# First stage of a hybrid decoder step: x in four column quarters, two weight groups in turn

## The reference

```python
def trunk_layer(x, lw, mlstm_fn, conv_fn):
    xn = rmsnorm(x, g_mix)
    z = xn @ w_in + b_in
    zq, zk, zv, zi, zf, zo, zu, zc, zb, zga, zgb = jnp.split(z, _split_points(), axis=-1)
    ...
    h, m_state = mlstm_fn(q, k, v, ig, lf)
    h_a = jax.nn.sigmoid(zo) * h
    conv_out, conv_state = conv_fn(zc * zu, w_conv)
    y_b = zb * conv_out
    merged = jax.nn.sigmoid(zga) * (h_a @ p_a) + jax.nn.sigmoid(zgb) * (y_b @ p_b)
    x = x + merged @ w_o
    u = jax.nn.relu(rmsnorm(x, g_ffn) @ w_up)
    x = x + (u * u) @ w_down
```

## Time and profile before

| | |
|---|---|
| Median of 3 runs | 1912.51 us (1912.1 to 1912.95) |
| Profiled execution, span | 1911.0 us |
| PE busy | 1889.9 us (99%) |
| PEld busy | 1855.8 us (97%) |
| DVE busy | 941.6 us (49%) |
| ACT busy | 689.5 us (36%) |
| Share of PE in the chain that ended last | 98% |
| PE busy in the first 20 us / the second 20 us | 9.12 us / 19.79 us |

### The profile page before, as it was taken

The page is one execution under the profiler, slowest core; times in us unless marked ns, Lnnn a source line. Parts: engine busy times, 40 slices in busy tenths (PEclk is TensorE's granted clock), DMA queues, the critical chain, the costliest instruction groups (busy, mean ns, idle before and its releaser), DMA issues.

```text
span 1911.0 us, 33610 instructions
## 1 busy us (share of the span) xinstructions
PE 1889.9 (99%) x12647; PEld 1855.8 (97%) x12647; DVE 941.6 (49%) x1045; ACT 689.5 (36%) x825; POOL 34.5 (2%) x67
## 2 busy tenths in 40 slices
PE   7999999999999999999999999999999999999998
PEld 7999898989899999999999999999999999999997
DVE  6565545454454444445555544455444544455544
ACT  5344343434343333333443333333333333333331
POOL 1001000010100000000000000000000000000000
PEclk9999999999999999999999999999999999999998
DMA  7446564756465545544454444444444444444442
GB/s 208 144 127 190 132 213 133 220 119 216 138 177 146 151 143 155 152 148 148 143 172 156 140 159 145 151 150 141 160 145 151 150 147 154 143 154 151 145 155 78
DMA packets 294469, 293.86 MB, mean 154 GB/s; under 512 B 12506, under 2 KB 292314, under 8 KB 294300
## 3 DMA queue, kind: packets, MB, share of 16 engines
q1 hardware_dynamic: 283464, 282.67, 48.8%
q10 hardware_dynamic: 10692, 9.51, 1.6%
q0 software_dynamic: 272, 1.12, 0.1%
HBM read 281.10 MB, written 12.17 MB: 153 GB/s over the span
## 4 chain that ended last, share of the span: by engine, by line
PE 98%; DVE 1%; DMA 0%; issue 0%; ACT 0%; SPq 0%; DVEq 0%; ACTq 0%
PE ps L1250 97%; DVE y_out L1243 0%; PE ps L1350 0%; DMA x_tok<-in_x_sample_dram 0%; PE ps L1270 0%; DVE x_low L840 0%; DVE x_T L843 0%; PE ps L1507 0%; DVE w_low L823 0%; ACT x_high L561 0%; PE ps L1451 0%; DVE sq_acc L1216 0%; DVE x_T L1212 0%; ACT tmp L790 0%; DVEq L110 0%
## 5 line engine op out<-in xcount | busy, mean ns | idle before, releaser
L823 DVE TENSOR_TENSOR w_low<-raw,w_high 128x1024 fp32r<-128x1024 f32 x512 | 621.7, 1226 | 609.0 <-ACT w_high L543 605.1
L543 ACT ACTIVATE w_high<-raw 128x1024 fp32r<-128x1024 f32 x512 | 534.9, 1055 | 712.5 <-PE ps L1250 709.1
L1250 PE MATMUL ps<-x_high,w_high 128*128 128x320 f32 (+2 forms) x2432 | 755.5, 311 | 1.3 <-PE ps L1250 1.1
L1250 PE MATMUL ps<-x_low,w_high 128*128 128x320 f32 (+2 forms) x2432 | 755.8, 311 | 0.0
L1250 PE MATMUL ps<-x_high,w_low 128*128 128x320 f32 (+2 forms) x2432 | 753.2, 310 | 0.0
L1250 PEld LDWEIGHTS ps<-x_high,w_high 128*128 128x128 f32 x2432 | 457.5, 188 | 7.2 <-issue 4.6
L1250 PEld LDWEIGHTS ps<-x_high,w_low 128*128 128x128 f32 x2432 | 458.6, 189 | 0.0
L1250 PEld LDWEIGHTS ps<-x_low,w_high 128*128 128x128 f32 x2432 | 457.3, 188 | 0.1
L1250 PE MATMUL ps<-u_high,w_high 128*128 128x320 f32 x1024 | 316.5, 309 | 0.0
L1250 PE MATMUL ps<-u_low,w_high 128*128 128x320 f32 x1024 | 316.4, 309 | 0.0
L1250 PE MATMUL ps<-u_high,w_low 128*128 128x320 f32 x1024 | 316.4, 309 | 0.0
(11 more groups left out here) (250 smaller groups left out, 1160.2 us busy)
## 6 DMA issues: line engine op xcount, KB each, us to landing
raw<-in_w_in_dram SPq DMA_DIRECT2D x176, 512.0 KB, 3.8
raw<-in_w_up_dram SPq DMA_DIRECT2D x128, 512.0 KB, 3.9
raw<-in_w_down_dram SPq DMA_DIRECT2D x128, 512.0 KB, 3.4
raw<-in_w_o_dram SPq DMA_DIRECT2D x32, 512.0 KB, 3.5
C_state<-in_state_mlstm_C_dram SPq DMA_DIRECT2D x16, 512.0 KB, 6.5
raw<-in_state_mlstm_C_dram SPq DMA_DIRECT2D x16, 512.0 KB, 4.1
out_dram<-C_state ACTq DMA_DIRECT2D x8, 1024.0 KB, 6.8
raw<-in_p_a_dram SPq DMA_DIRECT2D x16, 512.0 KB, 4.3
```

Source lines behind the costliest of these rows:

```text
L543: a.activation(wh[:, s % RING], raw[:, s % RING], ACT.Copy).then_inc(high_done, 1)
L823: v.tensor_tensor(wl[:, s % RING], raw[:, s % RING], wh[:, s % RING].bitcast(F32), ALU.subtract).then_inc(low_done, 1)
L1250: return pe.matmul(out, lhsT, rhs, start=start, stop=stop)
```

## The change

- SP loads x in four column quarters (672 KB each, five DMAs). Order: quarter 0, weights of units 0 and 1, quarter 1, units 2 and 3, quarters 2 and 3, units 4 and 5, the small rows, units 6 and 7. 
- The first convolution's units alternate: units 0 and 1 are row part 0 of zu and of zc, units 2 and 3 row part 1, and so on. Both accumulators are filled at the same time. XBANKS moves to the banks 4 to 7, the transposed vectors to ACC[0].
- PE: transposes of quarter 0, unit 0, transposes of quarter 1, units 1 and 2, quarter 2, units 3 and 4, quarter 3, units 5 and 6, columns, scales, unit 7.
- ACT: x_high of a quarter, splits and sums of squares in the written order below; its first instruction is x_high, no longer a sum.
- DVE: x_low of a quarter, then a split, then the plain copies x_T of that quarter.
- The four gate loads are issued by POOL instead of SP.

The diff, cut to its core:

```diff
@@ -230,7 +230,10 @@
         ACC = [ps[:, 0:2, :], ps[:, 2:4, :], ps[:, 6:8, :]]
         M = [ps[:, 4 + n, :] for n in range(4)]
         HEAD_ACC = [0, 1, 0, 1, 2]
-        XBANKS = [ACC[1], ACC[2]]
+        XBANKS = [ps[:, 4:6, :], ps[:, 6:8, :]]
+        XQ = 4
+        XB = KB // XQ
+        assert XQ == NU and XB == UK
 
         YPARTS = [(0, 0), (0, 1), (0, 2), (1, 0), (1, 1), (0, 3), (1, 2), (1, 3), (2, 0), (2, 1), (2, 2), (2, 3)]
         YBANK = [5, 6, 7, 0, 1, 2, 3]
...
@@ -361,10 +364,10 @@
 
         @block.sync
         def _(sp):
-            def tokens(half):
-
-                c = slice(D // 2 * half, D // 2 * half + D // 2)
-                in0, in1, in2 = s_xtok[3 * half:3 * half + 3]
+            def tokens(quarter):
+
+                c = slice(D // XQ * quarter, D // XQ * (quarter + 1))
+                in0, in1, in2 = s_xtok[3 * quarter:3 * quarter + 3]
                 sp.dma_start(xtok[0:NMETA, 0, c], meta[:, c]).then_inc(in0, 16)
                 sp.dma_start(xtok[NMETA:P, 0, c], x_prompt[0, 0:P - NMETA, c]).then_inc(in0, 16)
                 sp.dma_start(xtok[:, 1, c], x_prompt[0, P - NMETA:2 * P - NMETA, c]).then_inc(in1, 16)
...
@@ -391,15 +396,15 @@
                 sp.dma_start(crows[:], state_conv[0].rearrange("b r c -> (b r) c")).then_inc(s_brows, 16)
                 sp.dma_start(nrows[:], state_n[0].rearrange("b h d -> (b h) d")).then_inc(s_brows, 16)
 
-            def gates():
-                sp.dma_start(gw[:], w_in[0, :, CG:CG + 32].rearrange("(k p) n -> p k n", p=P)).then_inc(s_gw, 16)
-                with nc.allow_non_contiguous_dma(reason="40 numbers"):
-                    sp.dma_start(bi[:], b_in[0, CG:CG + H].rearrange("(h o) -> h o", o=1)).then_inc(s_small, 16)
-                    sp.dma_start(bf[:], b_in[0, CG + H:CO].rearrange("(h o) -> h o", o=1)).then_inc(s_small, 16)
-                    sp.dma_start(m0[:], state_m[0].rearrange("b h -> h b")).then_inc(s_small, 16)
-
             tokens(0)
-            convolution(0, {1: lambda: tokens(1), 3: small, 4: gates})
+            first_convolution(range(0, 2))
+            tokens(1)
+            first_convolution(range(2, 4))
+            tokens(2)
+            tokens(3)
+            first_convolution(range(4, 6))
+            small()
+            first_convolution(range(6, UCV))
             with sp.Fori(1, H) as i:
                 convolution(i)
             with sp.Fori(0, H) as h:
...
@@ -499,6 +511,7 @@
                 pool.wait_ge(s_pick, n + 2)
                 g.affine_select(out=pick[:], in_=pick[:], compare_op=ALU.not_equal, fill=1.0, base=-32 * n,
                                 pattern=[[-1, H]], channel_multiplier=1).then_inc(s_pick, 1)
+            gates()
             pool.wait_ge(s_row, 9)
             with nc.allow_non_contiguous_dma(reason="36 stabilisers"):
                 pool.dma_start(m_prompt.rearrange("l b h -> h (l b)"), mrw[:, TP - 1:TP]).then_inc(s_mout, 16)
@@ -545,26 +558,19 @@
             def sum_squares(half, n):
 
                 nt, done = (P, P, NMETA + TS)[n], 3 * half + n
-                act.wait_ge(s_xtok[done], 16 if n == 1 else 32)
+                for quarter in range(XQ // 2 * half, XQ // 2 * (half + 1)):
+                    act.wait_ge(s_xtok[3 * quarter + n], 16 if n == 1 else 32)
                 if done > 0:
                     act.wait_ge(s_sq, done)
                 a.activation(squares[0:nt, 0:D // 2], xtok[0:nt, n, D // 2 * half:D // 2 * half + D // 2], ACT.Square,
                              accum_out=spart[0:nt, half, n:n + 1]).then_inc(s_sq, 1)
 
-            act.wait_ge(s_set, 1)
-            for n in range(2):
-                sum_squares(0, n)
-
-            act.wait_ge(s_col, 1)
-            for k in range(KB):
-                act.wait_ge(s_xtr, k // 2 + 1)
-                a.activation(xh[:, k, :], XBANKS[k // 2 % 2][:, k % 2, 0:T], ACT.Copy,
-                             scale=vecT[:, VG + k:VG + k + 1]).then_inc(s_xh, 1)
-                if k % 4 == 3 and k // 4 < LEAD:
-                    split(0, k // 4)
-                    if k < 4:
-                        sum_squares(0, 2)
-                    sum_squares(1, k // 4)
+            def x_high(quarter):
+
+                for k in range(XB * quarter, XB * (quarter + 1)):
+                    act.wait_ge(s_xtr, k // 2 + 1)
+                    a.activation(xh[:, k, :], XBANKS[k // 2 % 2][:, k % 2, 0:T], ACT.Copy,
+                                 scale=vecT[:, VG + k:VG + k + 1]).then_inc(s_xh, 1)
 
             def root():
                 act.wait_ge(s_ms, 2)
...
@@ -611,7 +623,32 @@
                              ACT.Exp).then_inc(s_rowa, 1)
                 a.activation(wkr[:], wkr[:], ACT.Exp).then_inc(s_rowa, 1)
 
-            convolution(0, {1: root, 2: gate_weights, 3: lambda: act.wait_ge(s_col, 2)})
+            act.wait_ge(s_col, 1)
+            x_high(0)
+            split(0, 0)
+            split(0, 1)
+            x_high(1)
+            split(0, 2)
+            act.wait_ge(s_set, 1)
+            for n in range(3):
+                sum_squares(0, n)
+            split(0, 3)
+            x_high(2)
+            split(0, 4)
+            x_high(3)
+            split(0, 5)
+            for n in range(3):
+                sum_squares(1, n)
+            split(0, 6)
+            gate_weights()
+            split(0, 7)
+            root()
+            split(0, 8)
+            split(0, 9)
+            act.wait_ge(s_col, 2)
+            bias_u(0)
+            split(0, 10)
+            bias_c(0)
             with act.Fori(1, H - 1) as i:
                 convolution(i)
             convolution(H - 1, {1: log1p_exp, 4: row_exps})
...
@@ -835,14 +872,17 @@
                 dve.wait_ge(seen, n + 4)
 
 
-            for k in range(KB):
-                dve.wait_ge(s_xh, k + 1)
-                v.scalar_tensor_tensor(xl[:, k, :], XBANKS[k // 2 % 2][:, k % 2, 0:T], vecT[:, VG + k:VG + k + 1],
-                                       xh[:, k, :].bitcast(F32), ALU.mult, ALU.subtract).then_inc(s_xl, 1)
-                if k % 2 == 1:
-                    v.tensor_copy(xT[:, k - 1:k + 1, T0:T], XBANKS[k // 2 % 2][:, :, T0:T]).then_inc(s_xT, 1)
-                if k % 4 == 3 and k // 4 < LEAD:
-                    split(0, k // 4)
+            def x_low(quarter):
+
+                for k in range(XB * quarter, XB * (quarter + 1)):
+                    dve.wait_ge(s_xh, k + 1)
+                    v.scalar_tensor_tensor(xl[:, k, :], XBANKS[k // 2 % 2][:, k % 2, 0:T], vecT[:, VG + k:VG + k + 1],
+                                           xh[:, k, :].bitcast(F32), ALU.mult, ALU.subtract).then_inc(s_xl, 1)
+
+            def x_plain(quarter):
+
+                for k in range(XB * quarter, XB * (quarter + 1), 2):
+                    v.tensor_copy(xT[:, k:k + 2, T0:T], XBANKS[k // 2 % 2][:, :, T0:T]).then_inc(s_xT, 1)
 
             def columns():
                 dve.wait_ge(s_colT, 2)
@@ -884,14 +924,14 @@
             scale_z = rbc[:, TZ0:T].unsqueeze(1).to_broadcast([P, GB, TZ])
             scale_o = rbc[:, T0:T].unsqueeze(1).to_broadcast([P, GB, TO])
 
-            def convolution(i, extra=()):
-                for p in range(UCV):
+            def convolution(i, extra=(), begin=0, ends=(3, 7)):
+                for p in range(begin, UCV):
                     split(UCV * i, p + LEAD)
                     if p in extra:
                         extra[p]()
-                    if p in (3, 7):
-                        g = p // 4
-                        dve.wait_ge(unit_used, RING + UCV * i + 4 * g + 4)
+                    if p in ends:
+                        g = ends.index(p)
+                        dve.wait_ge(unit_used, RING + UCV * i + p + 1)
                         if g == 0:
                             dve.wait_ge(s_z, 1 + i)
                             dve.wait_ge(s_cv, 1 + 12 * i)
@@ -980,7 +1020,14 @@
                 row(v.tensor_copy(decr[:], rows[:, RWI:RWI + TS].rearrange("p (b t) -> p b t", t=DS)
                                   [:, :, DS - 1]))
 
-            convolution(0, {1: columns, 3: scales, 5: gate_weights})
+            for quarter in range(XQ):
+                x_low(quarter)
+                split(0, (0, 2, 4, 5)[quarter])
+                x_plain(quarter)
+                if quarter < 2:
+                    split(0, 2 * quarter + 1)
+            split(0, 6)
+            convolution(0, {4: columns, 5: gate_weights, 6: scales}, 4, (6, 7))
             with dve.Fori(1, H - 1) as i:
                 convolution(i)
             convolution(H - 1, {0: gates, 1: sums, 3: exponents, 4: decays})
...
@@ -1273,6 +1320,8 @@
 
             def columns():
                 pe.wait_ge(s_brows, 64)
+                pe.wait_ge(s_xl, KB)
+                pe.wait_ge(s_xT, KB // 2)
                 pe.transpose(M[0][:, 128:128 + nb], brows[:], ident[0:nb, 0:nb])
                 for k in range(CW // P):
                     pe.transpose(M[0][:, 256 + nc2 * k:256 + nc2 * (k + 1)], crows[:, P * k:P * k + P],
```

(39 more changed lines are left out.)

45 lines of the change are left out of this document (28 added, 17 removed).

## The result

The change makes the kernel slower: 1920.58 us in the median (1919.95 to 1922.36) against 1912.30 for the kernel before in the same set of runs, ratio 1.0044 with a 95% interval of 1.0032 to 1.0056. Measured again beside later kernels it was 1920.65 us, ratio 1.0051 (1.0038 to 1.0065). That is +8.3 us; the forecast was +9.9, to 1922.4.

The account below looks back on a forecast made before the run. PE, busy for 99% of the span, was taken as the bound. Terms -3.0 + 0.5 + 1.1 + 7.7 + 0.5 + 3.1 = +9.9 us gave a span of 1920.9, or 1922.4 us with 1.5 outside; range 1918 to 1926.

Parts of the forecast that it names:

- The start: Before unit 0: x in quarters lands earlier, table load adds 1.30 us; unit 0 at 13.2 instead of 16.19, -3.0 us.
- The turn: From a quarter's first transpose to the unit whose split stands behind x_high: 4.96 us, plus the table load at unit 0.
- Unit 0: In unit 0: PE's clock stays at its low level for 5.0 us instead of 3.9, +0.5 us.
- The waits: Between units 0 and 7: 0.4 at units 2 and 4, 3.8 unit 5, 0.8 unit 6, 3.0 scales; net +7.7 us.
- Unit 11: Behind unit 7: the split for unit 11 comes late after the delayed evacuation of the second group, +0.5 us.
- The falls: At the waits before unit 5 and the scales: PE's clock falls, 2.2 us each, together +3.1 us net.
- no fall or one fall: Rival: the clock falls once (1920.7 to 1921 us) or not at all (1919.3 us); chance 0.28.
- The collision of the gate weights: Rival: POOL's gate loads delay weight tiles, units 2 and 3 wait 2 to 3 us more, about 1925; chance 0.07.
- The doubled table load: Rival: ACT runs empty as long again behind the table load, 1.3 us more before unit 0, 1923.7 us; chance 0.05.
- that the waits don't occur: Rival: ACT and DVE run faster in the new order, waits under 5 us, clock stays up, about 1915; chance 0.08.
- The early start: Rival: the gain before unit 0 outweighs the losses elsewhere, 1908 us; chance 0.02.
- tau: In the waits' reckoning: the start of the transposes before the unit concerned, from which each time is counted.

Follow-up runs that it names:

- e6_table: Changed kernel with one tiny Square on ACT ahead of its wait for the column vectors, so the table load runs earlier: 1920.59 us, ratio 1.0046.
- f2_warm: f1_table with transposes of the identity into an unused bank before unit 0, to raise PE's clock early: 1909.73 us, ratio 0.9989.
- e9_hold: Changed kernel with PE kept at work by 24 products before unit 5 and 18 before the scales: 1920.44 us, ratio 1.0044.
- e8_sums: e3_both with ACT's second three sums of squares moved ahead of x_high of the last quarter: 1912.95 us, ratio 1.0004.
- e4_gates_late: Changed kernel with POOL issuing the gate weights' loads only after the last plain copies of x: 1921.43 us, ratio 1.0045.
- f1_table: e8_sums with the edit of e6_table, the table load ahead of x: 1912.11 us, ratio 1.0000.
- e3_both: Changed kernel with the edits of e1_unit5 and e2_norm together: 1916.12 us, ratio 1.0020.
- e1_unit5: Changed kernel with unit 5's split ahead of the last quarter's x_high and x_low, second sums still behind unit 6's split: 1916.99 us, ratio 1.0024.
- e2_norm: Changed kernel with DVE's chain for the norm ahead of the column copies, and those after the gate weights' split: 1916.74 us, ratio 1.0022.
- b1_before_warm: Kernel before the change with 26, 3 and 8 transposes of the identity added at its front: 1910.97 us, ratio 0.9993.
- e5_copies: Changed kernel with the x_T copies back after each two x_low, ahead of the unit's split on DVE: 1925.46 us, ratio 1.0069.

## Why the forecast was right, and where it was off

The forecast said slower, with a wait before unit 5, one before the scales and a fall of the clock at each, and that is what the trace shows. Step by step, by its own parts:

1. **The start, -3.0 forecast, -2.4 measured** (16.19 to 13.78). The shape was right: the table load stands before x_high, 8.30 to 9.58, and the activation begins at 9.60, as from the earlier trace rows. The drain of another 1.38 us that the Trainium skill adds to a load (ScalarE: Activation LUTs, section "What ACT_TABLE_LOAD costs") isn't there either; e6_table, which takes the load off the path, gains 1.1 us of wait, not 2.7. The mis-sized term was the landing. I had the first transpose of x at 6.3; it was at 6.86 and 7.17 in the two profiles, and up to 7.92 in other kernels with the same front. In the first profile it was not x that came last: its transposes follow that of the vector rows, at 6.68, without a break. The row names POOL, but by the program that transpose waits for the identity, which PE could use at 1.62 in f2_warm, and for the load of the vector rows, which the forecast took to be in by then. In the second profile it was x (idle 0.77 us, ended by its last load). The turn itself was 6.92 (6.86 to 13.78) against 6.9 forecast (6.3 to 13.2).
2. **Unit 0, +0.5 forecast, -0.15 measured.** The low level lasted 3.6 us in it (13.78 to 17.4; 2.8 in the second profile), not 5.0. The errors of this part and of part 1 cancel, which is luck: at the transposes behind unit 0 the forecast is -2.5, the trace -2.56.
3. **The waits.** Twelve transposes and 0.2 each at units 2 and 4 came as forecast. Unit 5: 3.8 forecast, 41.16 - 36.19 - 1.13 = 3.84 measured. Scales: 3.0 forecast, 2.93 measured. Unit 6: 0.8 forecast, 0 measured, as part 5 had said for the case of a fall; e9_hold shows it with 0.66 when the clock stays up. Program order and the durations of before were enough to get this part to 0.1 us.
4. **Unit 11, 0.5 forecast, 0 measured,** again hidden by the fall; e8_sums shows it with 0.50.
5. **The falls, +4.4 gross forecast, 3.2 measured,** two times 1.6. This is the term that was mis-sized: I took the 5.0 us from the start of the kernel for the length of a low stretch. Behind a hole in the middle of the work it was 3.4 us in both profiles of the changed kernel. With the 0.8 and the 0.5 that the falls hide, the forecast had 3.1 net, and the trace has 1.9. That a fall can last longer is shown by e4_gates_late, with 6.8 us; the forecast's upper bound had allowed 7.5.

From unit 1 to unit 12 the parts add up: 1.1 for the transposes, 0.4 at units 2 and 4, 3.8, 2.9, twice 1.6, less the 0.35 of before, gives 11.1 us; measured 53.76 - 42.77 = 11.0. With the front's -2.56 that is +8.4, and the medians differ by 8.3. The forecast's 9.9 is over by the 1.2 of part 5 and some tenths.

The rivals: no fall or one fall (0.28) is excluded by the windows view. The collision of the gate weights (0.07) is excluded by e4_gates_late. The doubled table load (0.05) is excluded by the activation at 9.60, and that the waits don't occur (0.08) by the timeline. The early start was worth 2.6 us at unit 1, against 11.0 behind it (12.9 forecast). The loads in quarters had no experiment of their own, but f1_table has them too and is level with the kernel before, so the 8.3 us are not theirs.

What the forecast did not see is how the repairs interact: that behind the norm's chain on DVE there was a second one on ACT which came due as soon as unit 5 was on time (e3_both). It could have been read from the forecast's own terms. The three sums behind the first split end at tau + 7.0; gate weights (0.3), a split (1.05) and the table load (1.28) put the root at tau + 9.6 and the diagonal 2 us behind it. With unit 5 on time PE comes to the scales at tau + 9.6 (47.30 - 37.72 in e3_both).

With all of it repaired (f1_table) the order in quarters stands even with the order in halves. The front gives 2.3 us (22.69 to 20.38), and the stretch behind it takes 2.6 us more than before (45.4 against 42.8): 1.1 for the twelve transposes that no longer lie in front of unit 0, 0.6 for three waits of 0.2, 0.3 before the scales, 0.5 at unit 11, the rest in hand-overs, less the 0.35 of before. The change moves work from where PE was waiting to where it was not.

## What to carry to other kernels

Where one engine is at its limit, read a new order of the others as a list: for each hand-over, what stands in front of it on the engine that delivers, and whether that could run earlier. A split of weights that have landed does not belong behind work that waits for something else; here two such places cost 6.6 us of waiting and 3.2 us of lowered clock, almost four times the 2.6 us that the earlier start won. And when two waits are removed, look for the third that was in their shadow: the gains of e1_unit5 and e2_norm alone, 3.6 and 3.9 us, gave 4.5 together until the next chain had been moved as well.

## What the runs showed of the hardware

- A hole of 2.46 us in steady work is enough to halve PE's clock (e3_both), and it fell behind three breaks of 1.13, 0.91 and 0.36 us with short work between them as well (b1_before_warm). It did not fall behind breaks of 0.97 and 0.37 us, close in front of unit 0 (f2_warm), and behind the 1.80 us in b1_before_warm twelve transposes still took 1.36 us, the full pace. The length of the idle time alone does not tell.
- The fall can come after the work has gone on: in e4_gates_late unit 5 began at 42.74 with matmuls 0.15 us apart, and only from 44.35 on they were 0.27 apart. The low stretch is not the same each time either: 3.4 us in the four falls of the two profiles of the changed kernel, 6.8 at the scales of e4_gates_late. Unit 5 took 5.16 us in the changed kernel and 5.70 in e5_copies.
- Transposes of the identity, which do no useful work, raise the clock. 26 of them took 4.76 us in b1_before_warm, 0.18 each in the mean, between the 0.21 at the low level (2.48 us for twelve of x) and the 0.11 at the high one (1.33), so it rose in their midst. In no kernel without them did it rise before unit 0 had run for 2.8 us.
- How far into unit 0 the clock rises varies from profile to profile, in kernels with the same front from 2.8 us (the changed kernel's second profile, unit 1 6.0 us behind unit 0) to 6.1 us (e4_gates_late, unit 1 7.5 us behind), which is 1.5 us of time. The Trainium skill (TensorE: Matmul & The Clock Gate, section "Part 1: The HAM clock gate") says that the point of the change varies from run to run, since the gate's view of the activity is not tied to the kernel's start. The profiles agree that it varies, and by more than the 0.5 us either way that the section gives. With the scatter of the first transposes of x (6.64 to 7.92) it makes it likely that four runs could not resolve 1 us in e6_table and e9_hold.
